# Depthwise convolution of a hybrid mixer: all four channel tiles on VectorE, GpSimd's share given up

## The reference

```python
def conformer_conv_branch(pc, dw_w, dw_b, ln_g, ln_b, w_pw, b_pw):
    c = pc[..., :CONV_CH] * jax.nn.sigmoid(pc[..., CONV_CH:])      # 512 channels
    c = causal_depthwise_conv(c, dw_w, dw_b)                       # 31 taps, one filter per channel
    c = jax.nn.silu(layer_norm(c, ln_g, ln_b))
    return c @ w_pw + b_pw
```

## Time and profile before

| | us |
|---|---|
| median of three runs | 2048.43 |
| lowest and highest | 2046.49, 2049.30 |
| the profiled execution's own time | 2047.05 |
| its span (first to last instruction) | 2045.3 |

### The profile page before, as it was taken

How to read it: one execution, slowest core, us unless ns; L and a number is a source line. 1 busy time by engine, 2 the same in 40 slices (tenths; PEclk the granted TensorE clock), 3 DMA queues, 4 the chain that set the end, 5 groups by cost and what they waited for, 6 DMA issues and landing times.

```text
span 2045.3 us, 26420 instructions
## 1 busy us (share of the span) xinstructions
PE 2009.9 (98%) x9850; PEld 1655.5 (81%) x9850; DVE 1225.3 (60%) x1374; ACT 1025.4 (50%) x1317; POOL 294.3 (14%) x365
## 2 busy tenths in 40 slices
PE   8999999999999999999999999999999999999998
PEld 6888888788888888887788887787778888788886
DVE  5555798864455455898855554556555555445554
ACT  5444686644435445586554454444444444455443
POOL 1000468200000000577200002111100000000000
PEclk9999999999999999999999999999999999999999
DMA  7554554455555555454455544443335554415552
GB/s 266 193 185 172 189 198 159 159 182 186 186 183 198 188 191 186 172 195 158 170 194 187 185 164 165 144 145 132 137 124 205 185 185 165 164 48 211 186 186 100
DMA packets 54626, 354.15 MB, mean 173 GB/s; under 512 B 7696, under 2 KB 8336, under 8 KB 12816
## 3 DMA queue, kind: packets, MB, share of 16 engines
q1 hardware_dynamic: 53968, 352.51, 48.1%
q10 hardware_dynamic: 576, 0.53, 0.1%
HBM read 351.97 MB, written 1.05 MB: 173 GB/s over the span
## 4 chain that ended last, share of the span: by engine, by line
PE 91%; DVE 3%; ACT 2%; DVEq 1%; issue 1%; DMA 0%; POOLq 0%; SPq 0%; ACTq 0%; POOL 0%
PE psum L1934 65%; PE psum L1985 17%; PE psum L2063 2%; DVE wlo L1094 1%; PE psum L2000 1%; PE psum L2403 1%; PE psum L2424 1%; DVEq L1349 1%; PE psum L2410 1%; PE psum L1946 1%; ACT whi L576 1%; PE psum L2111 0%; DMA raw<-w_stream 0%; PE psum L2140 0%; PE psum L2264 0%
## 5 line engine op out<-in xcount | busy, mean ns | idle before, releaser
L1094 DVE TENSOR_TENSOR wlo<-raw,whi 128x2048 fp32r<-128x2048 f32 x325 | 751.9, 2316 | 401.1 <-ACT whi L576 398.5
L1934 PE MATMUL psum<-whi,xTh 128*128 128x512 f32 (+1 forms) x1936 | 770.3, 398 | 5.6 <-DVE xTl L1111 4.9
L1934 PE MATMUL psum<-wlo,xTh 128*128 128x512 f32 (+1 forms) x1936 | 751.9, 388 | 0.0
L1934 PE MATMUL psum<-whi,xTl 128*128 128x512 f32 (+1 forms) x1936 | 751.7, 388 | 0.0
L576 ACT ACTIVATE whi<-raw 128x2048 fp32r<-128x2048 f32 x325 | 622.1, 1917 | 251.2 <-PE psum L1985 151.2
L1934 PEld LDWEIGHTS psum<-whi,xTh 128*128 128x128 f32 x1936 | 366.0, 189 | 83.0 <-issue 4.2
L1934 PEld LDWEIGHTS psum<-whi,xTl 128*128 128x128 f32 x1936 | 365.9, 189 | 76.3
L1934 PEld LDWEIGHTS psum<-wlo,xTh 128*128 128x128 f32 x1936 | 366.5, 189 | 68.4
L1985 PE MATMUL psum<-whi,braT 128*128 128x512 f32 x1056 | 337.9, 390 | 0.0
L1985 PEld LDWEIGHTS psum<-whi,braT 128*128 128x128 f32 x1056 | 198.2, 188 | 41.3
L1985 PE MATMUL psum<-wlo,braT 128*128 128x512 f32 x528 | 205.6, 389 | 0.0
(11 more groups left out here) (251 smaller groups left out, 1475.2 us busy)
## 6 DMA issues: line engine op xcount, KB each, us to landing
raw<-w_stream SPq DMA_DIRECT2D x326, 1024.0 KB, 4.8
bias<-chunks SPq DMA_DIRECT2D x18, 256.0 KB, 5.1
x<-x_in SPq DMA_DIRECT2D x2, 512.0 KB, 5.1
raw<-w_stream SPq DMA_DIRECT2D x4, 256.0 KB, 7.7
arena<-gate_w SPq DMA_DIRECT2D x2, 512.0 KB, 5.1
arena<-fins SPq DMA_DIRECT2D x2, 512.0 KB, 5.5
con<-consts SPq DMA_DIRECT2D x1, 720.0 KB, 11.2
out<-x ACTq DMA_DIRECT2D x2, 256.0 KB, 2.3
```

The costliest lines, as they stand in the source:

```text
L1094: TT(wlo[:, r], raw[:, r], whi[:, r].bitcast(F32), ALU.subtract).then_inc(lo_done, 1)
L1934: ins = pe.matmul(dst(rb), s(kt)[:, rows], w[:, r, at_:at_ + cols], start=start and n == 0 and k == 0, stop=stop and n == len(kts) - 1 and ...
```

## The change

`CONV_DVE` becomes 4. DVE's rounds have four instructions in place of three, and the sum of tile 3 lies in the second half of PSUM bank 5, which nothing else uses at that time. `taps` goes, with its two calls and PE's wait for `conv_pool`. Everything else, and the order of everything else, stays.

```diff
-CONV_DVE = 3
+CONV_DVE = 4
...
-                def taps(n):
-                    for k in range(done[0], done[0] + n):
-                        w, window = vec_("dww", k * 4 + CONV_DVE), cpad[:, CONV_DVE, k:k + S]
-                        if k == 0:
-                            TS(cacc[:, CONV_DVE], window, w, vec_("dwb", CONV_DVE), ALU.mult, ALU.add)
-                        else:
-                            TS(ctap[:, k % 2], window, w, None, ALU.mult)
-                        pool.drain()
-                        if k:
-                            ins = TT(cacc[:, CONV_DVE], cacc[:, CONV_DVE], ctap[:, k % 2], ALU.add)
-                        if k == TAPS - 1:
-                            ins.then_inc(conv_pool, 1)
-                    done[0] += n
...
                 wait(tdve, b.tdve + plan.upto("val1", "split", "dve"))
-                taps(11)
                 wait(lat_row, M + 1)
...
                 TT(gel, gr, gel, ALU.mult).then_inc(ya_f, 1)
-                taps(TAPS - 11)
                 with_conv_bias(0)
...
                     pe.wait_ge(conv_done, M + 1)
-                    pe.wait_ge(conv_pool, M + 1)
                     channel_mean(cacc, psum[:, 4, 0:S], mean_in)
```

More of the change, by code:

```diff
@@ L1772, in mix @@
                 rms(b)
-                done = [0]
-                def taps(n):
-                    for k in range(done[0], done[0] + n):
-                        w, window = vec_("dww", k * 4 + CONV_DVE), cpad[:, CONV_DVE, k:k + S]
-                        if k == 0:
-                            TS(cacc[:, CONV_DVE], window, w, vec_("dwb", CONV_DVE), ALU.mult, ALU.add)
-                        else:
-                            TS(ctap[:, k % 2], window, w, None, ALU.mult)
-                        pool.drain()
-                        if k:
-                            ins = TT(cacc[:, CONV_DVE], cacc[:, CONV_DVE], ctap[:, k % 2], ALU.add)
-                        if k == TAPS - 1:
-                            ins.then_inc(conv_pool, 1)
-                    done[0] += n
                 def with_conv_bias(c):
```

## The result

| | before | after |
|---|---|---|
| median, us (runs) | 2047.89 (6) | 2055.68 (6) |
| lowest to highest | 2046.49 to 2049.30 | 2054.15 to 2058.53 |
| profiled execution, its span | 2047.05, 2045.3 | 2054.34, 2052.6 |

The ratio after to before is 1.0039, with a 95% interval of 1.0027 to 1.0050: the changed kernel is 0.4% slower. The forecast was 2053.8, within 2049.3 to 2060.

The account below looks back on a forecast made before the run. PE, busy 98% of the span, bounds the kernel, so only DVE delays that make it wait count. Mixers lose 2.4 and 3.0 us: 5.4 over the median 2048.43 gives 2053.8, range 2049.3 to 2060.

Parts of the forecast that it names:

- The fourth instruction at 0.39 us: DVE's convolution rounds: each further instruction in a row adds 0.39 us, 31 of them 12.1 us per mixer.
- The relief: Early mixer: without GpSimd's taps, DVE's slowed short convolution and copies get 3.6 us back by 289.28.
- The slot at 291.75: PE's first use of the slot filled by the `wlo` of 289.28: 0.14 us of room, PE 0.6 late.
- The rotary wait: At 298.72 PE's 1.26 us wait for GpSimd's rotary products swallows its lateness; GpSimd 0 to 0.7 later, 0.3 taken.
- d: DVE's delay against before, followed down its list; forecast 0.3 us after the `wlo` at 298.64, behind round 14.
- The first pair: First pair of heads: seven rounds make DVE 2.8 us late at the reciprocals, PE's transposes lastingly 2.0 late.
- The chain: Chain of work ending last: again leaves PE at the third pair of heads (349.54 before), with the last rounds in it.
- The last rounds, first mixer: Rounds 28 and 29 hide in a 0.78 us gap before `o_lo`; 30 and 31 add 0.8; `wlo` at 366.18 gives 0.6 back.
- The second mixer: Repeats the first, but without the `wlo` and gated-bias overlap, so no 0.6 us back: 3.0 us in place of 2.4.
- DVE is not relieved: Rival: the short convolution is slow by itself, 10.8 us over before, 2059.2; no or half relief given 0.2.
- the second bias lets go: Rival: DVE's L1513 starts ahead of GpSimd's L1798, giving back 2.2 us per mixer, 2049.4; a flip or more gaps 0.23.
- nothing ends faster: Faster than before by over 0.2% (under 2044.3) needs that flip in both mixers and more relief than 3.6; chance 0.05.

Follow-up runs that it names:

- x1: Kernel before with GpSimd's taps left out and nothing in their place, so the fourth channel tile isn't convolved: 2047.80 us, ratio 0.9998.
- x6: Changed kernel with two of DVE's 31 rounds moved to where DVE waits for ACT, ahead of slots 22 and 24: 2048.13 us, ratio 1.0000.
- x10: Changed kernel with only one round moved, from ahead of the first pair's maxima to ahead of slot 22: 2052.40 us, ratio 1.0028.
- x12: Changed kernel unchanged, measured once more: 2054.83 us, ratio 1.0041.
- x3: Changed kernel with the DMAs of the last two gated-bias chunks issued one slot earlier: 2049.10 us, ratio 1.0006.
- x7: Changed kernel with both the two moved rounds and the earlier gated-bias DMAs: 2042.99 us, ratio 0.9975.
- x8: Kernel before, GpSimd's taps kept, with the two moved rounds and the earlier gated-bias DMAs: 2041.93 us, ratio 0.9971.
- x2: Kernel before with DVE convolving all four tiles and GpSimd's taps kept, their sum used by nobody: 2066.89 us, ratio 1.0092.
- x5: Changed kernel with a fifth instruction, both inputs in SBUF, in each of DVE's rounds but the first: 2081.92 us, ratio 1.0165.

## Why the prediction was right, and where it was wrong

The forecast was 5.4 us over before. The two medians are 7.8 apart, and the two profiled executions 7.3. The range held it. By its own steps:

**The fourth instruction at 0.39 us: right.** The row of four spans 1.66 us and the eight 3.42 and 3.40, as written down, and L1317 lasts 480 to 492 ns.

**The relief: right in kind, 3.9 for 3.6.** x1 shows it with nothing else changed. The whole came back, and not part of it. By the rule cited from the Trainium skill (SBUF — State Buffer, section on the two separate sides) it had to; the trace agrees, with L1366 at 475 to 487 ns in every place, and L1317, with one input in PSUM, at 479 to 492 with and without taps. L1364 was slowed too (four in 2.10 us, 1.38 without taps, for the 1.65 that I had taken), though it reads only one tensor; the rule as I cited it, on two inputs, doesn't speak of that case. And 0.5 us of the relief went into a new wait at 267.94, which I hadn't looked for.

**The slot at 291.75: right**, 0.65 late for 0.6 (0.9 from the entry), behind a `wlo` of 2.55 us.

**The rotary wait: wrong, to the good.** I had GpSimd up to 0.7 later there and took 0.3. But its first rotary product starts 0.21 earlier (285.57 for 285.78), which is no more than the 0.2 by which this execution entered the mixer early; it waits for ACT and not for the taps. With DVE's instructions at other places beside it, its last one ends another 0.16 earlier. PE begins at 298.35, 0.37 ahead of before. I had asked only what a late DVE does to GpSimd. The loss of 0.65 at the slot disappears in this, as forecast, and the 0.37 goes on to the `wlo` behind round 14, which ends 0.37 earlier: d = -0.4 for the 0.3 written down, or -0.15 from the entry.

**The first pair: right in size, by a neighbouring door.** From -0.4, seven rounds give 2.7, less 0.2, and the reciprocals are 2.2 late, 2.4 from the entry (forecast 2.8). I had this reach PE as 2.0 by way of the transposes. They are 0.7 late only. The lasting loss comes further on, in the scores of the second pair, where PE waits 0.75 us for `o_lo`, which DVE makes behind two more rounds: 2.06 us, 2.3 from the entry. x6 and x10, in which one round ahead of this goes elsewhere, bring it down to 0.5.

**The chain: wrong.** I had written that it would again leave PE at the third pair. It leaves PE at the `wlo` at 267.94 and is DVE's until those scores at 333.89. So in the changed kernel the whole of DVE's list between the two decides the time, and not only the part behind 349 us. (The chain before isn't off PE all the way from 349.54 to 407.60 either: it passes through PE for 2.8 us at 375.89.)

**The last rounds, first mixer: right.** The mixer costs 2.5, where the sum says 3.0 - 0.6 = 2.4. Of the cover of 0.78 before `o_lo`, 0.35 is left at 364.11.

**The second mixer: the step that failed.** The prediction says of it: "In the second there is no such overlap." The second mixer had no collision with the *first* bias instruction, but I went no further, to the *second*, which starts 0.25 us behind the end of the first. Before, `wlo` had started at 970.76, 0.31 ahead of it. DVE came 5.27 us later and GpSimd 4.63, a difference of 0.64, most of the 0.8 that the last two rounds had gained in length. So `wlo` started 0.33 behind, and paid 1.9 us, and the mixer cost 5.0 and not 3.0. The sum without this term is 2.4 + 3.0 = 5.4. With it, 7.3, and the spans are 7.3 apart. I had named a flip between these two engines as a rival and priced it at 2.2, but looked for it only at L1513, where it would have been a gain. This one is at another place, and has the other sign.

**The rivals.** That DVE is not relieved was refuted by x1. That the second bias lets go did not happen in the profile of the changed kernel (L1513 3.43 and 3.42). In the second mixer of x12, the same kernel, it did (1.21), but the `wlo` before it paid 1.9 for it. x3 brings it about in both mixers, and gets 4.4 of its 6.6 us by it. That nothing ends faster was right for this order of the list; with the two edits of x7 the changed kernel does, but so does the kernel before (x8).

**Two misses among the experiments.** x2 was dearer than its expectation, and so was x5. They fail in the same way: I added delays up to a place at which I had seen a gap, and used a gap again that the fourth instruction had already filled. The cushion had been of one size, about 9.6 us in a mixer, and counted once. For x2 that is in part argued, as its profile is of an execution far above its median.

**What stays open.** The 1.1 us between x7 and x8 are not told apart from nothing. Which way the first mixer's tie falls in the longest executions of the changed kernel no trace shows. In x5 only the 11.7 us per mixer of plain length is accounted for; the other 1.4 is the collisions, waits of PE and its clock in some proportion. Why PE's clock fell in the mixers of x2, x5 and x12, and not in those of the changed kernel's first profile, is not shown.

## What to carry to other kernels

An engine at 60% over the span can have no room at the one place that matters: follow the delay down its list, gap by gap, and count each gap once. Work taken off an engine that shares a port is worth only what fills the time it frees (0 us in x1, 11.2 in x2 against after). Before adding a little work to a list, look where its later instructions run beside another engine's long ones with a start within a microsecond: there a shift of 0.64 us of one engine against the other cost 1.9, and moving two rounds and two DMAs gave back 12.7. When two executions are compared instruction by instruction, take off what they differ by on entry: here it was up to 0.65 us, as large as some of the terms.

## What the runs showed that I had not expected

**At the shared port a lead of a few hundredths of a microsecond is enough, and the loser pays for the whole instruction.** `wlo` ahead by 0.05 us lasts 2.28 and leaves GpSimd at 4.49; behind by 0.33, it lasts 4.19 and GpSimd 2.37. From the first start to the last end the pair takes 4.5 us either way. Which of the two stands on the chain decides whether it costs anything: `wlo` does, and GpSimd's bias here doesn't.

**A GpSimd instruction of full width stops even a small one of VectorE with two inputs in SBUF** for all its remaining length: 2.56 us for an instruction of 0.48 in x5. The same operation with its sum in PSUM was never over 493 ns in any of the traces, with taps beside it (x2, before) or without. This choice of the depthwise convolution, made for all four tiles, kept the 12.1 us from growing; the fifth instruction of x5, without it, was held up for 2.6 us in the first mixer.
